# The 32 later ada_w loads move from GpSimd's DMA queue into SyncE's, between the weight loads of the first block

## The reference, cut to what matters

```python
c_act = silu(c)                               # one row of 1024
mod = c_act @ ada_w + ada_b                   # ada_w is 1024 x 6144
sh1, sc1, g1, sh2, sc2, g2 = split(mod, 6)    # six vectors of 1024
h = rms_norm(x, norm1_g) * (1 + sc1) + sh1
proj = h @ w_in + b_in                        # w_in is 1024 x 2304: q, k, v, gb, gc, xs
...                                           # rope, windowed attention, a gated 3-tap convolution
x = x + g1 * (y @ w_o)                        # w_o is 1024 x 1024
h = rms_norm(x, norm2_g) * (1 + sc2) + sh2    # and then the feed-forward part, with g2 at its end
```

## Time and profile before

| | |
|---|---|
| time, median of 3 runs | 2205.49 us (2201.45 to 2206.65) |
| the profiled execution's own time | 2201.45 us |
| its span in the profile | 2199.7 us |
| TensorE busy | 2020.3 us, 92% |
| VectorE busy | 1079.6 us, 49% |
| ScalarE busy | 785.0 us, 36% |
| GpSimd busy | 230.8 us, 10% |
| TensorE's granted clock, mean | 0.953 of full speed |

### The profile page before, as it was taken

How to read it: one execution, slowest core, us unless ns; L and a number is a source line. 1 busy time by engine, 2 the same in 40 slices (tenths; PEclk the granted TensorE clock), 3 DMA queues, 4 the chain that set the end, 5 groups by cost and what they waited for, 6 DMA issues and landing times.

```text
span 2199.7 us, 35366 instructions
## 1 busy us (share of the span) xinstructions
PE 2020.3 (92%) x14391; PEld 1579.3 (72%) x14391; DVE 1079.6 (49%) x1571; ACT 785.0 (36%) x1243; POOL 230.8 (10%) x263
## 2 busy tenths in 40 slices
PE   7998989999996988799988899999889779999997
PEld 5776768888871666577766688888768557888885
DVE  6767765554227343677743644432253644444323
ACT  4335233333222333576634333322243433222221
POOL 1100000000013000222211011110000011111100
PEclk8989989999998999799989999999989889999998
DMA  8544223333321222000002133333123022333320
GB/s 291 173 126 122 87 66 90 93 95 110 103 73 33 67 77 68 7 10 8 7 25 77 55 98 95 95 111 100 57 77 95 19 68 86 95 95 99 114 83 39
DMA packets 311051, 181.00 MB, mean 82 GB/s; under 512 B 16381, under 2 KB 303763, under 8 KB 310932
## 3 DMA queue, kind: packets, MB, share of 16 engines
q1 hardware_dynamic: 305506, 162.29, 25.2%
q0 software_dynamic: 4608, 16.78, 2.5%
q10 hardware_dynamic: 818, 0.21, 0.0%
HBM read 177.16 MB, written 2.10 MB: 81 GB/s over the span
## 4 chain that ended last, share of the span: by engine, by line
PE 85%; DVE 8%; ACT 3%; issue 2%; SPq 1%; DMA 0%; POOL 0%; DVEq 0%; ACTq 0%
PE bank L247 23%; PE bank L248 22%; PE bank L249 22%; PE bank L1884 4%; DVE rstd L351 2%; PE bank L441 1%; PE bank L333 1%; PE bank L2365 1%; SPq L214 1%; PE bank L2359 1%; PE bank L2466 1%; ACT whi L226 1%; DVE tmp L1234 1%; SPq L505 1%; PE bank L1098 1%
## 5 line engine op out<-in xcount | busy, mean ns | idle before, releaser
L232 DVE TENSOR_TENSOR wlo<-raw,whi 128x1024 fp32r<-128x1024 f32 (+1 forms) x262 | 340.3, 1299 | 777.2 <-ACT whi L226 777.0
L226 ACT ACTIVATE whi<-raw 128x1024 fp32r<-128x1024 f32 (+1 forms) x262 | 293.1, 1119 | 784.7 <-PE bank L249 777.2
L247 PE MATMUL bank<-fh_hi,whi 128*128 128x512 f32 x1056 | 420.7, 398 | 26.9 <-DVE fh_lo L415 19.4
L248 PE MATMUL bank<-fh_lo,whi 128*128 128x512 f32 x1056 | 414.9, 393 | 0.0
L249 PE MATMUL bank<-fh_hi,wlo 128*128 128x512 f32 x1056 | 414.8, 393 | 0.0
L247 PEld LDWEIGHTS bank<-fh_hi,whi 128*128 128x128 f32 x1056 | 199.1, 189 | 84.5 <-DVE fh_lo L415 29.9
L248 PEld LDWEIGHTS bank<-fh_lo,whi 128*128 128x128 f32 x1056 | 199.2, 189 | 44.6 <-issue 2.2
L249 PEld LDWEIGHTS bank<-fh_hi,wlo 128*128 128x128 f32 x1056 | 199.1, 189 | 44.1
L248 PE MATMUL bank<-f_lo,whi 128*128 128x512 f32 x528 | 205.6, 389 | 0.0
L247 PE MATMUL bank<-f_hi,whi 128*128 128x512 f32 x528 | 205.6, 389 | 0.0
L249 PE MATMUL bank<-f_hi,wlo 128*128 128x512 f32 x528 | 205.6, 389 | 0.0
(11 more groups left out here) (399 smaller groups left out, 3060.2 us busy)
## 6 DMA issues: line engine op xcount, KB each, us to landing
raw<-in_w_up_dram SPq DMA_DIRECT2D x44, 512.0 KB, 3.8
raw<-in_ffn_w_gate_dram SPq DMA_DIRECT2D x44, 512.0 KB, 3.8
raw<-in_ffn_w_up_dram SPq DMA_DIRECT2D x44, 512.0 KB, 3.8
raw<-in_ffn_w_down_dram SPq DMA_DIRECT2D x32, 704.0 KB, 4.6
late<-in_ada_w_dram POOLq DMA_DIRECT2D x32, 512.0 KB, 4.1
raw<-in_rwkv_w_rkv_dram SPq DMA_DIRECT2D x24, 512.0 KB, 4.0
raw<-in_w_down_dram SPq DMA_DIRECT2D x16, 704.0 KB, 4.6
early<-in_ada_w_dram SPq DMA_DIRECT2D x16, 512.0 KB, 14.1
```

Source lines behind the costliest of these rows:

```text
L226: act.activation(whi[:, at.slot, 0:kts * P], raw_unit(at, kts), ACT.Copy).then_inc(hi_ready, 1)
L232: dve.tensor_tensor(wlo[:, at.slot, 0:kts * P], raw_unit(at, kts), whi[:, at.slot, 0:kts * P].bitcast(F32), ALU.subtract).then_inc(lo_read ...
L247: pe.matmul(dst, hi, rhs_hi(k), start=first and k == 0, stop=False)
L248: pe.matmul(dst, hi, rhs_lo(k), start=False, stop=False)
```

## The change

`pool_late` is gone, and GpSimd no longer calls it. Its 32 DMAs are issued by SP instead, in one hand-written order with the 26 units: after in0 panels 16 and 17, after in1 18, after in2 19 and 20, after in3 21, after in4 22 and 23, and so on to in11. Then one panel follows each unit up to o7. Their waits are the same as before. But they now stand in SP's program, ahead of the units that come behind them.

```diff
+    order, m = [], EARLY
+    for u in range(N_IN):
+        order.append(("in", u))
+        for _ in range(2 - u % 2 if u < 12 else 1):
+            order.append(("late", m))
+            m += 1
+    for u in range(N_O):
+        order.append(("o", u))
+        if m < 6 * KD:
+            order.append(("late", m))
+            m += 1
...
-        for kind, n, at in seq:
+        for kind, n, at in plan:
+            if kind == "late":
+                if n == EARLY:
+                    sp.wait_ge(x_turned, KD)
+                if n >= EARLY + RAW:
+                    sp.wait_ge(*ada_used(n - RAW))
+                sp.dma_start(late[:, n % RAW, :], ada_rows(n)).then_inc(late_landed[n % RAW], 16)
+                continue
             freed = None
...
-    def pool_late(pool):
-        pool.wait_ge(x_turned, KD)
-        for n in range(EARLY, 6 * KD):
-            if n >= EARLY + RAW:
-                pool.wait_ge(*ada_used(n - RAW))
-            pool.dma_start(late[:, n % RAW, :], ada_rows(n)).then_inc(late_landed[n % RAW], 16)
...
         pool_setup(pool)
-        pool_late(pool)
         norm_f.pool_sum(pool)
```

More of the change, by code:

```diff
@@ L452, in build @@
     EARLY = 2 * KD
-    at_in, at_o, seq = {}, {}, []
[L454 to L459, removed]
+    order, m = [], EARLY
[9 more added lines that the diff above has]
+            m += 1
+    at_in, at_o, seq = {}, {}, []
+    u_next, plan = 0, []
+    for kind, n in order:
+        at = None
+        if kind != "late":
+            at = At(len(seq), u_next)
+            seq.append((kind, n, at))
+            {"in": at_in, "o": at_o}[kind][n] = at
+            u_next += 1
+        plan.append((kind, n, at))
     first = [at for _, _, at in seq]
```

## The result

The changed kernel takes 2223.06 us in the median of four runs (2221.89 to 2225.13) against 2205.31 for before (four runs, 2201.45 to 2206.65). The ratio is 1.0085, with a 95% interval from 1.0066 to 1.0102: 17.75 us slower by the medians. The ratios here are worked out from all runs and not from two medians (whose quotient is 1.0080 here); one run, of the kernel with the changed order from in9 on, took 2469.19 us at a granted clock of 0.776 and is left out of its median and ratio. The profiled execution took 2221.25 us, its span 2219.5.

The account below looks back on a forecast made before the run. TensorE was taken to bound the kernel (busy 92% of the span), VectorE close behind in the q, k, v units. Terms -0.2 + 15.7 = +15.5 us on 2205.49 gave 2221.0 us, range 2211 to 2229.

Parts of the forecast that it names:

- opening: Before the sum of `mod`: late panels no longer compete with in0, gain at most about 0.2 us, taken as -0.2.
- in3: Unit 3's load waits behind panel 20 for panel 16's sum; ScalarE's split 6.4 us later, at 65.5 us.
- in4: Unit 4's load stands behind panel 21, which waits for the sum of 17; costs 4.8 us.
- in5: Unit 5's load stands behind panel 23, which waits for the sum of 19; costs again 4.8 us.
- in6 and in7: In6 there when wanted; in7 behind panels 25 and 26, landing at 100.2 us; together -0.3 us.
- The price of a landing behind one panel: Unit load on SP's queue lands 5.1 us after issue, ends 4.0 and 5.9; appears four times in the sum.
- one of my own signs of being wrong: Prediction named itself wrong if, among other signs, landings behind a panel take 4 us or 7.
- Why it ends at in7: From in8 on, units are wanted an attention step or more after the releasing sum: 7 us upwards against 5.6 needed.
- only in3 would be held up: Rival at the q, k, v units: SP catches up after in3, giving 2208 us; chance 0.09.
- the opening would win: Rival before `mod`: both VectorE waits go, 2.6 us, and later waits do not bite, 2202.9 us; chance 0.03.
- Half clock: Rival at units 4, 5 and attention: idle TensorE drops to 1.2 GHz, 1.5 to 5 us more; chance 0.25.
- The ring: Units 4 and 5: rotation and sum, SP's answer and panel issue, landing, two splits; 11.1 us per turn against 6.35.

Follow-up runs that it names:

- the first experiment: All 32 panels on SP's queue, each moved behind units whose slots are free by then, against the kernel before: 2203.12 us, ratio 0.999.
- The second experiment: Against the changed kernel, GpSimd issues the panels as before and SP only makes the waits at the same places: 2217.06 us, ratio 1.0062 to before.

## Why the prediction was right

The sign, the mechanism and the place were right. Forecast was 2221.0, measured 2223.06. Term by term, from one split of ScalarE to the next in the changed kernel against before:

| term | forecast, us | measured, us | how |
|---|---|---|---|
| opening | -0.2 | about 0 | `mod` at 42.60 to 43.49 or 46.05 to 46.37, whatever the order |
| in3 | +6.4 | +6.6 | 9.32 against 59.13 - 56.41 = 2.72 |
| in4 | +4.8 | +4.7 | 11.06 against 6.35 |
| in5 | +4.8 | +4.6 | 10.94 against 6.35 |
| in6 and in7 | -0.3 | +1.9 | 91.00 to 105.56 is 14.56; forecast 12.5; before 84.52 - 71.83 = 12.69 |
| sum | +15.5 | +17.8 | |

**The opening.** The argument that TensorE's matmuls cap the gain held; the first experiment shows VectorE's waits gone and TensorE's in their place. The wait on `x_turned` cost nothing, as forecast: SP issued panel 16 at 27.62, right behind in0. That the opening can come out 3 us longer by itself was not foreseen. The profile of before has the short one and the first profile of the changed kernel the long one. How many of the timed runs had the long one is not known, so part of the nearness of 2221.0 to 2223.06 may be luck.

**The first three hold-ups.** The chain of steps is as written, and its durations agree within 0.3 us. The price of a landing behind one panel, taken from five loads of before at 5.1 us, was 5.35 for in3's second half, 5.12 for in4 and 5.00 for in5. That price was the part bound loosest, from 4.0 to 5.9. In its rows the panel goes out on GpSimd's queue about 1 us ahead, here on SP's own queue 0.4 us ahead. The prediction did not weigh this difference; that the price carried over was not argued.

**In7, the term that was mis-sized.** I wrote that in7 stands behind panels 25 and 26 and still gave it 5.1 us. It landed in 7.3, and in four of the experiments' profiles in 7.4, 6.9, 7.3 and 7.2, each time with two panels issued within 2 us of it, and in 5.0 and 4.9 with one ahead. Those 2.2 us are nearly all of the 2.3 that the sum missed. The rows behind my price have one panel each ahead of them, and I used them for a place with two. A landing of 7 us behind a panel was one of my own signs of being wrong, and for in7 it came true. I also said that in6 would be on the chip when wanted. It landed in 7.2 us as well, with three loads issued in the 1.8 us before it, and ScalarE waited 1.97 us for it. But VectorE was busy with sums until 97.88, after ScalarE's split of in6 (94.59 + 1.06 = 95.65), and the second of these sums is what in7's panel waited for, so this cost nothing. The term's -0.3 is itself rounded to make the sum meet: 10.1 against 10.3 is -0.2.

**Why it ends at in7.** As argued, and shown by the kernel with the changed order from in9 on. That everything behind it is as before holds too: from in8's split to the end of the span the profiles take 2199.7 - 99.35 = 2100.35 us before and 2219.5 - 120.70 = 2098.80 in the changed kernel, and the ten profiles lie between 2098.8 and 2103.1.

**The rivals.** That only in3 would be held up is out: three further splits wait over 9 us. That the opening would win is out. Half clock came, as the rival said, in more places than the first scores, but cost next to nothing. Busy time by stretch in the changed kernel, units 4 and 5 and the first attention step:

```profile
82.00:86.00 4.00, 4.00 (x8) 2.49 (x9) 3.86 (x6) 0.00 (x0) 0.00 (x0) 0.50 0.00 0
94.00:97.00 3.00, 3.00 (x8) 2.32 (x7) 2.86 (x4) 1.63 (x2) 0.00 (x0) 0.50 0.00 1
110.00:114.00 4.00, 4.00 (x12) 3.10 (x13) 2.79 (x10) 1.27 (x6) 0.00 (x0) 0.50 0.43 129
```

TensorE stood idle for 4.46 us before unit 4 and 1.92 before unit 5, where 4 to 5 us before each was forecast. In the first of these waits the granted clock fell to half, 1.2 GHz, where it had been full all the time before the change. It rose at about 86.8, fell again at about 93.6 and rose at 97.0. So TensorE worked at half clock for some 8.4 us, which made its busy time about 4.2 us longer. The ring took that up: TensorE was done with unit 4 at 90.76, still 1.92 us before it could go on. This bears on a number of the prediction. The busy share of TensorE was to fall to near one half between 59 and 100. It fell to 0.76 (31.01 of 41.00 us from 62.3 to 103.3, the same stretch behind the later opening). The prediction's own unit starts give four units of 6.35 us in 41, 0.62, and the half clock adds 0.1.

At the first attention step the half clock is on the path, and it was before the change. Between the splits of in7 and in8 TensorE did about 5.3 us of its work at half clock, 3.4 before, and that interval is 15.14 us (120.70 - 105.56) against 99.35 - 84.52 = 14.83 before: 0.3 us more, and not 1.5 to 5. It does not stay so small by itself. In the first experiment TensorE did about 6.0 us of work there at half clock, and the interval was 15.96.

**The fit against the rows.** The prediction weighed the fit of the Trainium skill, "DMA: Bandwidth & Descriptors", Anatomy of one DMA, against the rows. By it a unit would land 4.4 us after the issue of the panel ahead of it, an estimate by that page. In the changed kernel it took 80.06 - 74.53 = 5.5 us, where 74.53 is when SP issued panel 21. The rows were nearer, and the sum by the page, +10.7, would have been 7 us short. The same page says, in the same section, that a semaphore wait is made by the issuing sequencer before it sends the DMA off. The second experiment shows what that means here: a wait with no DMA behind it held up every load after it.

## What to carry to other kernels

Before a DMA goes into another queue, write down what it waits for and what stands behind it. If the wait is for an engine that itself waits, however far down the line, for something behind it in that queue, the queue has closed a ring, and each turn costs the whole ring (here 11.1 us for a unit of 6.35) and not the few tenths of the issue. The cure is not a faster queue but order: put the waiting DMA behind all that can go earlier. Then the same queue carries it for nothing that was measurable here (ratio 0.999, 0.9977 to 1.0003).

When a duration is taken from other rows, match what was in flight just before them: none, one or two 512 KB loads just ahead made 4.0, 5.1 and 7.3 us of the same load here.

## What the runs showed of the hardware

- A 512 KB load of this kernel landed in 7.3 us when two others were issued 1.8 and 0.4 us before it in its own queue, and in 7.4 us when GpSimd issued two, 1.2 us before it and 0.2 us after it. With one panel 0.4 us ahead and another 1.0 us behind it landed in 5.0.
- SP issued a 128 x 4 KB load in 0.33 us (median of 32) where GpSimd took 0.53. In the opening, right behind the 16 early panels, single issues of SP took up to 3.8 us for a panel and 9.2 us for one half of in0; a full queue would explain it, but no run shows that.
- The opening of this program has two lengths about 3 us apart, in ten profiles seven times the shorter. In the three long ones the granted clock fell to 1.2 GHz while the 32 products with early panels ran, in the others after them.
